# Background steps placed by clocks of three engines, finer waits at block-diagonal products and conv evictions, and modulation tiles spread in the queue, in a two-block float32 model

## The reference

```python
for l in range(DEPTH):
    h = rms_norm(x, norm_mix_g[l])
    a_x, a_y, m_u, m_o, m_i, m_f, xa_q, gate_pre = split_columns(h @ w_in[l])
    xa_c = causal_dwconv(a_x, conv_rg_w[l], conv_rg_b[l])
    y_rg = rg_lru(xa_c, ...) * gelu(a_y)          # two block-diagonal products of 4 blocks of 256
    y_ml = mlstm_branch(m_u, m_o, m_i, m_f, ...)  # conv, three block-diagonal products, 4 heads
    y_xa = memory_attention(xa_q, rms_norm(mem, ...), w_kv[l])
    merged = sum(sigmoid(gate) * (y @ w_br) for the three branches)
    x = x + merged @ w_out[l]
    x = x + (swiglu(...) if l % 2 == 0 else moe_swiglu(...))(rms_norm(x, norm_ffn_g[l]))
```

## Time and profile before

| | us |
|---|---|
| median of the runs | 3647.12 |
| the profiled execution | 3649.55 |
| its span, first to last instruction | 3647.8 |
| TensorE busy | 3357.4 |
| VectorE busy | 2337.5 |
| ScalarE busy | 1849.9 |

### The profile page before, as it was taken

How to read it: one execution, slowest core, us unless ns; L and a number is a source line. 1 busy time by engine, 2 the same in 40 slices (tenths; PEclk the granted TensorE clock), 3 DMA queues, 4 the chain that set the end, 5 groups by cost and what they waited for, 6 DMA issues and landing times.

```text
span 3647.8 us, 56528 instructions
## 1 busy us (share of the span) xinstructions
PE 3357.4 (92%) x24411; PEld 3080.7 (84%) x24411; DVE 2337.5 (64%) x2986; ACT 1849.9 (51%) x2198; POOL 0.2 (0%) x4
## 2 busy tenths in 40 slices
PE   7979999989689899999999999898799979998798
PEld 7968989989689799999999999775577869974598
DVE  6756655567566588888888888534465545555354
ACT  5454444445544377777776776423444434434343
POOL 0000000000000000000000000000000000000000
PEclk9989999999899899999999999997799989999899
DMA  6423455444234599899899998323224355411253
GB/s 248 163 86 114 171 211 193 173 162 152 93 116 171 200 372 352 330 353 349 329 360 336 342 360 324 129 78 127 104 87 157 127 198 184 174 59 58 93 185 116
DMA packets 102671, 723.49 MB, mean 198 GB/s; under 512 B 11664, under 2 KB 13328, under 8 KB 16528
## 3 DMA queue, kind: packets, MB, share of 16 engines
q1 hardware_dynamic: 102416, 719.80, 53.2%
HBM read 718.71 MB, written 1.05 MB: 197 GB/s over the span
## 4 chain that ended last, share of the span: by engine, by line
PE 80%; DVE 9%; ACT 6%; DMA 3%; issue 1%; SPq 0%; DVEq 0%; ACTq 0%
PE PS L1361 14%; PE PS L1362 13%; PE PS L1363 13%; PE PS L1314 6%; PE PS L1312 6%; PE PS L1313 6%; DVE WL L2064 3%; PE PS L1618 3%; PE PS L1616 3%; PE PS L1617 3%; ACT WH L1680 3%; PE PS L1428 3%; PE PS L1457 2%; DMA RAW<-in_ffn_w 1%; PE PS L1391 1%
## 5 line engine op out<-in xcount | busy, mean ns | idle before, releaser
L2064 DVE TENSOR_TENSOR WL<-RAW,WH 128x2048 fp32r<-128x2048 f32 (+3 forms) x428 | 962.9, 2252 | 646.7 <-ACT WH L1680 641.5
L1680 ACT ACTIVATE WH<-RAW 128x2048 fp32r<-128x2048 f32 (+3 forms) x428 | 802.7, 1878 | 270.3 <-PE PS L1363 182.0
L1361 PE MATMUL PS<-PH,WH 128*128 128x256 f32 x2464 | 715.5, 290 | 34.8 <-DVE PL L2236 11.1
L1362 PE MATMUL PS<-PL,WH 128*128 128x256 f32 x2464 | 700.9, 284 | 0.0
L1363 PE MATMUL PS<-PH,WL 128*128 128x256 f32 x2464 | 700.7, 284 | 0.0
L2064 DVE TENSOR_TENSOR WL<-F,WH 128x2048 fp32r<-128x2048 f32 x210 | 481.2, 2292 | 87.5 <-ACT WH L1680 86.5
L1361 PE MATMUL PS<-HPH,WH 128*128 128x256 f32 (+1 forms) x1648 | 496.9, 302 | 41.7 <-DVE WL L2064 27.1
L1361 PEld LDWEIGHTS PS<-PH,WH 128*128 128x128 f32 x2464 | 475.3, 193 | 43.8 <-issue 29.8
L1362 PE MATMUL PS<-HPL,WH 128*128 128x256 f32 (+1 forms) x1648 | 482.4, 293 | 0.0
L1363 PE MATMUL PS<-HPH,WL 128*128 128x256 f32 (+1 forms) x1648 | 482.3, 293 | 0.0
L1362 PEld LDWEIGHTS PS<-PL,WH 128*128 128x128 f32 x2464 | 475.2, 193 | 1.3
(11 more groups left out here) (379 smaller groups left out, 5158.4 us busy)
## 6 DMA issues: line engine op xcount, KB each, us to landing
F<-in_moe_w SPq DMA_DIRECT2D x210, 1024.0 KB, 5.1
RAW<-in_ffn_w SPq DMA_DIRECT2D x130, 1024.0 KB, 4.8
RAW<-in_moe_w SPq DMA_DIRECT2D x126, 1024.0 KB, 4.9
RAW<-in_w_in SPq DMA_DIRECT2D x64, 1024.0 KB, 4.8
F<-in_ada_w SPq DMA_DIRECT2D x18, 1024.0 KB, 11.2
RAW<-in_ada_w SPq DMA_DIRECT2D x18, 1024.0 KB, 5.9
RAW<-in_w_kv SPq DMA_DIRECT2D x16, 1024.0 KB, 4.7
RAW<-in_w_in_ab SPq DMA_DIRECT2D x12, 1024.0 KB, 4.9
```

Source lines behind the costliest of these rows:

```text
L1361: T_.matmul(out, lh, rh, start=first, stop=False)
L1362: T_.matmul(out, lh, rl, start=False, stop=False)
L1680: S.activation(mem["WH"][:, t.s % NHL, 0:m], v.raws[t.slot][:, 0:m], ACT.Copy).then_inc(*ac.done("w_hi", t.s))
L2064: V.tensor_tensor(mem["WL"][:, t.s % NHL, 0:m], v.raws[t.slot][:, 0:m], mem["WH"][:, t.s % NHL, 0:m].bitcast(F32), sub).then_inc(*dv.done( ...
```

## The change

`put` now keeps an estimate of the time at which VectorE and ScalarE are done (`busy`), from a table of durations by unit (`work`), and returns when the unit is done by all of them; its argument `after` says when it can begin. `bank` returns when the bank's last user is done with it. A chain now yields an absolute time, that of the result which its next step needs, and `weave` offers it a step from then on. Plan time also waits: for a bank, for a tile's low part (`open`), for what a step needs. Lanes rise from 3 to 5 beside og and mu, the memory heads have four buffers for turned probabilities instead of two, the rows go in 8 steps instead of 4.

The block-diagonal products wait for the conv block of their own pair, and their banks turn round in all 8 (`fgc`). The low part of u is made directly behind the conv on VectorE instead of in `cvd`. The six modulation tiles behind wo of layer 0 are queued in pairs between the first three tiles of the feed-forward, all of them behind the four wo tiles. In layer 1 the last wo tile splits one tile less ahead. The feed-forward of layer 0 changes the buffers of its groups (p1, p2 instead of p2, p1), runs c2 tile 0, then c3, then c2 tiles 1 to 3, and the application of mem1 is cut in steps: the scaling beside group 3, high and low parts beside c2 tiles 1 and 2.

```diff
@@ class Plan
+    def put(self, *unit, cost=0.0, after=0.0):
         self.units.append(unit)
-        self.clock += cost or COST.get(unit[0], 0.0)
+        cost = cost or COST.get(unit[0], 0.0)
+        if cost:
+            self.clock = after = max(self.clock, after) + cost
+            after += 0.1
+        for engine, us in work(self, unit):
+            self.busy[engine] = after = max(self.busy[engine], after) + us
+        return after + 0.05
...
+def work(p, unit):
+    kind, *args = unit
+    if kind == "tile":
+        return ((A, 1.85), (V, 2.21))
...
+        if kind == "e":
+            return ((V, 0.3 + 0.27 * wide + 0.15 * swa), (A, 0.15 + 0.25 * wide + 0.25 * swa))
+        if kind == "n":
+            m = args[2]
+            return ((V, 0.25 + 0.2 * wide + 0.15 * swa + 0.3 * m),)
...
+    if kind == "row":
+        return (((V, 1.5), (A, 0.4)), ((V, 2.3),), ((V, 2.1),), ((V, 1.7),), ((V, 1.7),), ((V, 2.5),), ((V, 1.2),), ((V, 2.6), (A, 0.4)))[args[1]]
+    if kind == "napp":
...
+        return ((V, 6.4), (A, 0.4), (V, 0.8)) if "gn" in p.norms[args[0]] else ((V, 5.2), (A, 0.55), (V, 0.7))
...
+    def open(self, g, t, ahead=NHL):
+        n = self.tile[g.name, t].s
+        self.split_at[n + 2] = self.put("tile", (g.name, t), ahead)
+        self.clock = max(self.clock, self.split_at.get(n, 0.0))
...
-                        yield 0.8 if roomy and m < members - 1 else 1.5
+                    yield at[some[0]]
...
-                        self.put("e", name, qb, m)
+                        at[m] = self.freed_at["s", name, qb, m] = self.put("e", name, qb, m, after=at[m])
...
+                    if some[-1] == members - 1:
+                        yield scaled
+                free = self.bank(("t", name, qb), self.bgc)
+                copied = self.freed_at["t", name, qb] = self.put("t", name, qb, cost=u, after=max(free, scaled))
...
-            wait = next(c.steps, None)
-            if wait is None:
+            c.at = next(c.steps, None)
+            if c.at is None:
                 self.live.remove(c)
-            else:
-                c.at = self.clock + wait
@@ def first_order(p):
+        p.fgc = ALL
         p.lin_all(L("rga", "diag", "tanh_r", io["rg_w_a"][l], 0, 256, p1, ready=cv))
         p.lin_all(L("rgx", "diag", "tanh_i", io["rg_w_x"][l], 0, 256, p1, ready=cv))
+        p.fgc = FG
...
-        p.lanes = 3
+        p.lanes = 5
...
         for t in range(4):
-            p.lin(wo, t, p.follow(f"f{l}"))
-            if t == 3 and l == 0:
-                p.modulation(3, [8, 4, 5, 6, 9, 3], [("ps", f"br2_{l}", 7)])
+            p.begin(wo, t)
+        if l == 0:
+            first = swiglu_ahead(p, "ffn", io["ffn_w1"][0], io["ffn_w3"][0], h, T, norm="f0")
+            p.modulation(1, [8, 4], [("ps", f"br2_{l}", 7)])
+            p.begin(*first[0])
+            p.begin(*first[1])
+            p.modulation(1, [5, 6])
+            p.begin(*first[2])
+            p.modulation(1, [9, 3])
+        for t in range(4):
+            p.lin(wo, t, p.follow(f"f{l}"), 2 if l and t == 3 else NHL)
@@ def swiglu_order (with along)
+    p.lin(second[0], 0)
+    p.lin(second[1], 0, after)
+    for t in range(1, 4):
+        p.lin(second[1], t)
+    def both(i):
+        after(i)
+        if i < 6:
+            along(i - 2)
+    for t in range(1, 4):
+        p.lin(second[0], t, both)
@@ tensor_program, lin
         for ready in g.ready:
-            pe.wait_ge(*ready)
+            pe.wait_ge(*(ready[:2] + (i - i % 2 + 1,) if g.form in ("diag", "dtok") else ready))
@@ vector_program, lin, conv_ml (moved here from cvd)
+                V.tensor_tensor(u.l[:, i, :], ps[:, 0:T], u.h[:, i, :].bitcast(F32), sub).then_inc(*dv.done("cv_lo", name, i, "u"))
+                dv.frees(name, i)
```

309 lines of the change are left out of this document (193 added, 116 removed).

## The result

The changed kernel takes 3545.49 us in the median (3542.19 to 3550.56), the kernel before, run beside it, 3647.01. The ratio is 0.9717, with a 95% interval of 0.9704 to 0.9731. The profiled execution took 3550.56 us, its span is 3548.7.

A forecast was written before the change was run, and what follows sets the result against it. TensorE's own work and its 290.4 us of standing still, plus clock loss, were taken as the bound. Terms 31 + 24 + 4 + 7 + 2 + 7 + 12 = 87 us gave 3560 us, eight in ten between 3505 and 3650.

The forecast's parts named there:

- (a): Memory heads and rows, both layers: transposes wait less when steps are placed by engine clocks; 31 us for both.
- (b): Block-diagonal products, both layers: finer waits and eight banks remove waits and some clock loss; 24 us, bounds 8 and 29.
- (c): rga in layer 0: a shorter wait before it, eight banks for rgx included; 4 us, bounds 1 and 13.
- (d): Modulation tiles spread in layer 0's queue: first ffn tile lands sooner, 7 us; layer 1's last tile, 2 us.
- (e): Turn to layer 1: mem1's application no longer delays c3's additions on VectorE; 7 us, bounds 0 and 10.
- (f): Second block: few dense products between steps, so order wins little; 12 us won, bounds 35 won and 25 lost.
- R1: All comes, every step where its data are ready: (a) 62, (b) 29, (f) 35, (c) 10; 3495 us, 10%.
- R2: Heads stay as late as they are, ScalarE's queue sets the pace, (a) and (f) give nothing; 3603 us, 18%.
- R3: Slower: plan time runs ahead of the chip and transposes come too early; 3695 us, 12%.
- R4: Gaps shrink but the low clock stays, so some 20 to 25 us don't come back; 3583 us, 15%.
- the sign that (c) is wrong: At rga: a wait for L2236 of 10 us still there, or gone altogether.

The follow-up runs named there:

- blind_first: The changed kernel, but the plan knows no durations of VectorE and ScalarE in the first block up to the experts; 3603.64 us, ratio 0.9878.
- edits_without_clocks: The kernel before, with only waits by pairs of conv blocks, eight banks for block-diagonal products and u's early low part; 3635.57 us, ratio 0.9969.
- modulation_tiles_in_one_piece: The changed kernel, with layer 0's modulation tiles queued in one piece behind wo's tiles, ahead of the first ffn tiles; 3553.29 us, ratio 0.9742.
- Fixed_waits_second_block: The changed kernel, but the second block's attention heads wait by the old fixed numbers instead of the engines' clocks; 3588.86 us, ratio 0.9835.
- before_fewer_fills: The kernel before, with filling modulation products at most every 9 us of plan time instead of 6; 3672.93 us, ratio 1.0071.
- longer_durations: The changed kernel, with every VectorE and ScalarE duration in the plan times 1.3; 3556.59 us, ratio 0.9736.

## Why the prediction was right, and where it was not

I said 3560 us, it became 3545.5. For the profiled execution I had a sum of 87 us and 3562.6; it saved 99.0 us. The mechanism is right, steps that come late because the list doesn't know the queues of VectorE and ScalarE; two sizes came near by luck, as the points show.

**(a) and (b), heads and block-diagonal products.** I had 31 and 24 for both layers, 55 in all; heads to gate saved 26.8 + 22.8 = 49.6 us. The sum was near, the split was wrong, and so was a reason; that 27 us too little and 33 too much cancel almost is luck. Og/mu alone saved 58.3, close to the upper bound of 62, not the half that I took. Not all of it is the clocks' work: 48.0 come in blind_first too, and are then lost again in the next stages. I had halved it for table loads that five mixed chains would bring. In the stage there were ten before silu and exp and two more before the exp of the rows, twelve in all. The two more, and behind them the five of ScalarE in the same stage of after:

```profile
L1852 ACT ACT_TABLE_LOAD x1 | 1.3, 1283 | 0.0
L1855 ACT ACT_TABLE_LOAD x1 | 1.3, 1283 | 0.0
...
L1924 ACT ACT_TABLE_LOAD x2 | 2.6, 1283 | 0.0
L1975 ACT ACT_TABLE_LOAD x1 | 1.3, 1283 | 0.0
L1936 ACT ACT_TABLE_LOAD x1 | 1.3, 1283 | 0.0
L1978 ACT ACT_TABLE_LOAD x1 | 1.3, 1283 | 0.0
```

Four exp steps now stand side by side, so the table changes at most once for four. So the premise under which I weighed the Trainium skill's price of a load (ScalarE: Activation LUTs, What ACT_TABLE_LOAD costs) against the change was wrong: by either price fewer loads speak for it. For (b) the block-diagonal stretch saved 3.7 and 4.2 us and the next stage gave 7.2 and 9.3 back. There the gate's dense products had to cover more steps. TensorE's waits in 266 to 347 us of after:

```profile
PE PS L1638 <- DVE F L2510: 3.9, 1, 3.9
PE PS L1484 <- DVE F L2304: 2.8, 1, 2.8
```

L2510 is a step in the chain of an mLSTM head (`ml`, step 2), L2304 the eviction of mv, for whose bank the first gate product waits; I had expected the gate's weight tile to be late next. All kernels with the clocks and the true durations give 7 to 11 us back here; the edits without clocks give back 1.6 and 1.5. I conclude that the return comes from the placing: og/mu is shorter, and VectorE's work, 119.7 us in the three stages before and 119.8 after, has less time in them (197.5 us before, 170.7 after). That VectorE's order in the gate is the whole cause wasn't tried.

**(c), rga of layer 0.** I had 4 us with bounds of 1 and 13. Rga started 7.6 us earlier, and 3.5 of them were left behind rgx, 1.7 at og/mu. The size was near by luck, the step was wrong: I took the low part made from 84.52 us on the earlier trace rows for rga's own tile. It is rgx's. Rga's tile stands one further up in VectorE's timeline of before:

```profile
73.19 2.29 DVE L2064 TENSOR_TENSOR WL<-RAW,WH 128x2048 fp32r<-128x2048 f32 x1
```

It was finished at 75.5, so the finer wait alone could bring rga forward by 10 us and not by 0.9; edits_without_clocks did that, with 10.3. The gain doesn't last, but not for the low part of the last pair: TensorE doesn't wait for it in after. It is ScalarE that sets the end. It copies the high parts of two tiles first, the second until 87.8 us, and then evicts rga. The first eviction before, the first one after, and the first product behind rgx in after, which waits for rgx's evictions:

```profile
89.39 0.48 ACT L1750 ACTIVATE F<-PS,PAR 128x256 f32<-128x256 f32 x1 [0.83 <-PE PS L1363]
87.72 0.47 ACT L1873 ACTIVATE F<-PS,PAR 128x256 f32<-128x256 f32 x1
99.72 0.55 PE L1484 MATMUL PS<-PH,WH 128*128 128x256 f32 x1 [3.48 <-ACT F L1881]
```

ScalarE starts only 1.7 us earlier and needs 1.0 us for each of the eight items, so TensorE's earlier start comes to stand behind it. The wait for L2236 is gone altogether, which I had named as the sign that (c) is wrong.

**(d), the tiles in the queue.** 8.3 us for 7, with the cause shown by modulation_tiles_in_one_piece. Layer 1's part was 2 us; from wo to the end of the experts 1.4 were saved, but only 0.1 and 0.4 in two other kernels with the same list there, so it isn't shown.

**(e), the turn to layer 1.** 8.7 us for 7, in a stretch that saves 8.4 to 10.6 in every kernel that has the change's order of c2 and c3, and loses 0.8 with the other edits alone. Its parts weren't taken one by one.

**(f), second block.** This is the term that was mis-sized: 33.6 us for 12, near the bound of 35, and 37.0 to 41.7, beyond it, in the five other kernels with the same second block. I argued that few dense products stand between the steps, so that order wins little. Fixed_waits_second_block shows 44 us for the dates. And the fear that `fill` would put more modulation products into the first attention stage had the wrong sign: five came, not more than seven. Why plan time that waits asks for fewer wasn't tried. What I priced right was that they are missing later, but not how dear: 13 us net by the trace of before_fewer_fills, 27 by its medians.

**The rivals.** R1 gave 152 us, from (a) 62 and (f) 35, both of which came, plus (b) 29 and (c) 10, which didn't. R2 fell, since og/mu saved 58. R3 fell: the transposes' waits behind VectorE's scaling went from 61.7 us to 5.8 for PQ and none for F. R4 fell: the clock is at 0.960, and 32.7 us of busy time came back, where I had counted 20 to 25. Where I had built R4 it is right, though: over the first attention stage and the one behind it (2428.98 to 2666.20 us before, 2364.40 to 2570.68 after) the clock rose only from 0.80 to 0.82.

The ledger closes: 87 + 21.6 (f) - 5.4 (a, b) - 2.3 (c) + 1.3 - 0.6 (d) + 1.7 (e) - 4.2 (small losses at the other gates, at the start of layer 1 and in the rest of it) = 99.

## What to carry to other kernels

When a program's order is written by hand or by a planner, give the planner the queues of all engines, not only of the bound one; durations 30% too long cost 5 to 11 us of the 100 here, while with no durations and no waits in their place the same structure was worth nothing in the first block. Judge a moved background step over all the stages in which its chain runs, since a gain in one was given back in the next, by a quarter to a third in after and almost wholly without durations. And look at the DMA queue last: four lines that put weight tiles ahead of tiles that are needed later were worth 31 us more, a third of what the whole change brought.

## What the hardware showed that I had not expected

A wait that is removed is worth more or less than its length. In og/mu of layer 0 removing 22.4 us of idle time brought 8.0 more on the same 466 products, whose granted clock rose from 0.84 to 0.98. At rga a wait of 10 us could be put back at a cost of 0.3, since ScalarE's evictions set the end there. A bank can be such a wait too: eight banks in place of four let rga run into a bank that VectorE frees 5.3 us later.

One modulation product, of 2.9 us at the clock of that stage (11.61 for four), cost 10.6 us in the last attention stage (31.8 for three), 2.4 of them by the clock of the other products; with longer_durations, which has none there, it was 6.4 (25.5 us for four), with before_fewer_fills 10.1 (20.2 for two more). TensorE was busy 83% of the stage at a granted clock of 0.87 with four of them, and 84% at 0.94 with one; the busy share alone didn't tell the clock.
